# Sixteen more token rows through gathered down rows, and every second lower weight block split on VectorE

## The chip, the cores and the metric

The kernel runs on one core of a Trainium2 chip. Its time is device microseconds of one execution; before the change the median of three runs is 1582.86 us (1582.15 to 1584.1). The profiled execution took 1584.32 us, of which 1582.4 us lie between its first and its last instruction.

## The reference

One decoder layer over 512 tokens of width 1024: a mixer, cross-attention into 256 memory tokens, and a PEER channel mixer, in which each of 8 heads chooses 16 of 16384 single-neuron experts for every token. Nearly all that matters here is the last part:

```python
q = (tokens @ w_query).reshape(Ntok, PEER_HEADS, 2, PEER_DK)
s = jnp.einsum('nhpd,hpkd->nhpk', q, sub_keys)
s_top, i_top = lax.top_k(s, K)                       # K = 16 in each half
cand = (s_top[:, :, 0, :, None] + s_top[:, :, 1, None, :]).reshape(Ntok, PEER_HEADS, K * K)
best, pos = lax.top_k(cand, K)
gate = jax.nn.softmax(best, axis=-1)
u = jnp.take(expert_down, idx, axis=0)
a = jax.nn.gelu(jnp.einsum('nd,nhkd->nhk', xb, u), approximate=False)
v = jnp.take(expert_up, idx, axis=0)
out = jnp.einsum('nhk,nhkd->nd', gb * a, v)
```

## The kernel before, in words

The tokens lie in four tiles of 128. Up to the queries all four are treated alike. In the channel mixer the work is split by tokens.

**Dense tokens.** For the first three tiles without their last 32 rows (352 tokens, the constant DE) nothing is gathered. The products with all 16384 down rows are made, in 128 blocks of 128 experts, each 24 matmuls of 352 columns (8 chunks of the width, three products of a split into a high and a low half). GELU is applied to all of them, a dense table of gates, zero for what isn't chosen, multiplies them, and 128 blocks of the up matrix follow, again 24 matmuls of 352 columns each.

**Gathered tokens.** The fourth tile, and the 32 last rows of the third (the edge), fetch the rows that they chose, one token to a partition. A gather brings 128 rows (512 KB); the fourth tile needs 128 of them, the edge 32, with 4 slots to a token. VectorE then makes one dot product of each gathered tile with the tokens (the function dots, line 1250, result in dot3 or edge_dot).

**The stage of down blocks** is where the change works. It has three parts. In the first, 52 blocks (AHEAD), TensorE makes down blocks while VectorE chooses the experts of the three dense tiles, with dots in between: 18 to a tile, 54 in all. In the second, 44 steps (STEPS), each step is one block and one gate step of 24 small matmuls from one-hot tables that VectorE builds (the function hots); DOTS_STEP gives the dots of each step, 74 in all. In the third, the last 32 blocks, DOTS_END gives the dots still open, 32, one to a block for 22 blocks and then two.

**The order on each engine** is written out by hand. A down block passes through four engines: SyncE loads it into a ring of 5, ScalarE rounds it into a high half in a ring of 3 (the function high, line 603), GpSimd subtracts to get the low half (the function low, line 470), and TensorE waits for the low half (the function columns). Since the high ring has three places, ScalarE splits block i+2 only when block i-1 has been used, which is when block i begins. ScalarE also writes the GELU of each block (line 853, and line 952 for the last 24 blocks, which stay in SBUF; the others go out to DRAM and come back).

GpSimd does two things in one program order: the low halves, and the issue of the gathers (the function down_row, line 502). In the first part the tiles of gathered rows are a ring of 7, and GpSimd issues them at a set pace of 6 for 5 blocks. From the second part on the ring has 4 places, so gather k waits until dot k-4 is done, and GpSimd issues the gathers of block i right after the low half of block i, so that the last gather that it issues there needs the last dot that VectorE makes in the matching step.

ScalarE waits for VectorE's choice before blocks 15, 30 and 45 (EXP_AT), and TensorE turns the chosen numbers before blocks 36 and 51 (turn_indices).

**The stage of up blocks** has 128 blocks. VectorE multiplies the hidden values by the gates: 320 columns from a table that came back from DRAM (line 1474) and 32 from a table kept in SBUF (near, line 1478).

Of the kernel before, what the change touches and what calls it, by code (L numbers as in the profile page):

```python
# [8 lines left out]
U32 = mybir.dt.uint32  # L9
# [34 lines left out]
EXP_AT = (15, 30, 45)  # L44
PICKED_AT = 19
TURN_AT = (PICKED_AT + 4, 36, 52)
# [3 lines left out]
DE = DN - EDGE  # L50
STEPS = DE // TB
# [14 lines left out]
ROWS = SLOTS + EDGE_SLOTS  # L66
FIRST_EDGE = 32
LOWS = range(33, 40)
GEL_AT, SPLIT_AT, LAST_TURN = 12, 20, 28
# [17 lines left out]

def row_stream():
    stream, own, edge = [], 0, 0
    for k in range(ROWS):  # L90
        if edge < EDGE_SLOTS and k >= FIRST_EDGE:
            stream.append((True, edge))
            edge += 1
        else:
            stream.append((False, own))
            own += 1
    return stream
# [3 lines left out]
EDGE_DONE = FIRST_EDGE + EDGE_SLOTS  # L101

# [5 lines left out]
def build(nc, x_in, mem_in, vecs_in, final_in, ffn_in, front_w, keys_in, down_in, down_rows, up_in, up_pairs, out, gate_dram, hid_dram):  # L108
    ctx = ExitStack()
    with ctx:  # L110
# [110 lines left out]
        hid = [at(kb, DE) for kb in (137.25, 138.625, 18.5, 19.875)]  # L221
        hk_last, split_last = at(136.25, 2 * P, 2, P), at(26, 3 * P, 3, P)
        edge_idx, edge_dot, edge_gel = (at(kb, EDGE_SLOTS) for kb in (18, 18.125, 18.25))
        edge_gate, edge_w, edge_sum_of = (at(17.5 + 0.125 * j, EDGE_SLOTS) for j in range(3))
# [27 lines left out]
        hid_kept = [at(kb, DE) for kb in [108 + 1.5 * j for j in range(4)] + [156 + 1.5 * j for j in range(10)]  # L252
# [6 lines left out]
        hidr = at(60, 2 * PAIRS_IN * DE, 2 * PAIRS_IN, DE)  # L259
# [7 lines left out]
        low_ready = sem("low_ready")  # L267
# [53 lines left out]
        edge_moved, fin_squares = sem("edge_moved"), sem("fin_squares")  # L321
        mix_square, mix_last = sem("mix_square_of_third_tile"), sem("mix_last_tile")
# [123 lines left out]
        def _(pool):  # L446
# [45 lines left out]
            def down_row(k):  # L492
# [6 lines left out]
                edge, j = STREAM[k]  # L499
                if edge and j == 0:  # L500
                    pool.wait_ge(edge_moved, 2 * 16 * PARTS)
                nc.gpsimd.indirect_dma_start(ring[slot], None, down_rows, bass.IndirectOffsetOnAxis(  # L502
                    (edge_idx if edge else idx3)[:, j:j + 1].bitcast(U32), 0))\
# [59 lines left out]
        def _(act):  # L563
# [44 lines left out]

            def weight_high(i, s):
                act.wait_ge(w_raw, i * 2 + 2)  # L610
                nc.scalar.activation(wgt_half[0][:, s, 0:DE], wraw[:, s, 0:DE], ACT.Copy).then_inc(w_high, 1)
# [234 lines left out]
            def early_at(i):  # L846
# [6 lines left out]
                nc.scalar.activation(hid[i % HIDS], psum[:, 4 + i % 2, 0:DE], ACT.Gelu).then_inc(gelu_out, 1)  # L853
                act.wait_ge(gelu_out, i + 3)
                act.dma_start(hid_dram[i // 2, :, i % 2 * DE:(i % 2 + 1) * DE], hid[i % HIDS])\
# [23 lines left out]
            for n in range(DT):  # L879
                early_tiles((4 + PARTS, TURN_AT[0], TURN_AT[1])[n], EXP_AT[n])  # L880
# [10 lines left out]
                elif n == 1:  # L891
                    early_tiles(EXP_AT[n], TURN_AT[n])
# [15 lines left out]
            for n in range(STEPS):  # L908
# [3 lines left out]
                if n == GEL_AT:  # L912
                    act.wait_ge(dot_done, EDGE_DONE)
                    step(nc.scalar.activation(edge_gel, edge_dot, ACT.Gelu))
                    act.wait_ge(idx_ready, 3)
                if GEL_AT <= n < GEL_AT + PARTS:
# [25 lines left out]
            for j in range(KEEP):  # L942
# [9 lines left out]
                nc.scalar.activation(hid_kept[j][:, 0:DE], psum[:, 4 + i % 2, 0:DE], ACT.Gelu).then_inc(gelu_out, 1)  # L952
                if i == NK - 4:
                    act.wait_ge(dot_done, ROWS)
                    high_up(0, 0, 16)
# [4 lines left out]
                if i == NK - 2:  # L960
                    high_up(1, 1, 16)
                    weight_high(1, 1)
            for s in range(2, 4):
                high_up(s, s, 16)
                weight_high(s, s)
            for u in range(4, RING_U):
                act.wait_ge(up_done, u - 3)
                high_up(u, u, 16)
                weight_high(u, u % 4)
            with act.Fori(1, NK // RING_U) as r:  # L970
                for s in range(RING_U):
                    act.wait_ge(up_done, r * RING_U + (s - 3))
                    high_up(r * RING_U + s, s, r * 16 + 16)
                    weight_high(r * RING_U + s, s % 4)
# [37 lines left out]
        def _(dve):  # L1012
# [221 lines left out]
            def dots(first, count):  # L1234

                for k in range(first, first + count):
# [5 lines left out]
                    edge, j = STREAM[k]  # L1242
# [7 lines left out]
                    nc.vector.tensor_tensor_reduce(ring[slot], ring[slot], h_row, 1.0, 0.0, ALU.mult, ALU.add,  # L1250
                                                   (edge_dot if edge else dot3)[:, j:j + 1]).then_inc(dot_done, 1)
# [168 lines left out]
            for n in range(STEPS):  # L1420
# [4 lines left out]
                if n == SPLIT_AT:  # L1425
# [3 lines left out]
                                                     ident.rearrange("p (q t) -> p t q", q=PARTS), AX_X, ALU.add))  # L1429
                    step.end()  # L1430
# [5 lines left out]
            kd = dots(kd, ROWS - kd)  # L1436
# [29 lines left out]
            def weigh(i, landed, block, kept_hid=None):  # L1466
# [4 lines left out]
                else:  # L1471
# [7 lines left out]
                    wraw[:, s, FAR * CH:DE].rearrange("p (i n) -> p i n", i=1),  # L1479
                    h[:, FAR * CH:DE].rearrange("p (i n) -> p i n", i=1),  # L1480
                    near[:, block:block + 1, :], ALU.mult).then_inc(w_raw, 1)
# [65 lines left out]
        def _(pe):  # L1547
# [45 lines left out]
            def columns(b, rhs, n, bank):  # L1593

                pe.wait_ge(low_ready, b + 1)
# [447 lines left out]
```

## Time and profile before

| what | value |
|---|---|
| median of three runs | 1582.86 us |
| profiled execution | 1584.32 us |
| its span, first to last instruction | 1582.4 us |
| TensorE busy | 1565.8 us, 99% |
| VectorE busy | 1164.6 us, 74% |
| GpSimd busy | 963.6 us, 61% |
| ScalarE busy | 663.3 us, 42% |
| moved by DMA | 438.91 MB |

The profile shows one execution. PE is TensorE's matmuls, PEld its weight loads, DVE is VectorE, ACT ScalarE, POOL GpSimd, SP SyncE. A matmul's busy time is longer than its share of the array, since matmuls overlap: what one costs is read from the distance between starts. A time in square brackets behind a row is the idle time of that engine before it, and the name behind it is what ended it. psum, kept and arena are the large memories: kept and arena hold nearly every tile, so rows are told apart by their line.

### The profile page before, as it was taken

To read this page: it belongs to the slowest core of one execution; us is meant where nothing else is said; L and a number is where in the kernel's file an instruction comes from. 1 tells how busy PE (TensorE), PEld (TensorE's weight loads), DVE (VectorE), ACT (ScalarE), POOL (GpSimd) and SP (SyncE) were. 2 spreads that over 40 slices of the span, in tenths; PEclk is the share of its full clock that TensorE was granted. 3 is DMA by queue.
4 is the path that set the end of the run, shared out by engine and by line. 5 is a ranking of instruction groups with operands and counts; after the bars stand their busy time and mean duration, and the time that the engine had idled before them with its cause. 6 is when DMAs were issued, how large, how long until landed. Compare 5 with 4: busy or idle time off the path is not lost.

```text
span 1582.4 us, 26079 instructions
## 1 busy us (share of the span) xinstructions
PE 1565.8 (99%) x9937; PEld 1483.6 (94%) x9937; DVE 1164.6 (74%) x2263; ACT 663.3 (42%) x994; POOL 963.6 (61%) x555
## 2 busy tenths in 40 slices
PE   8999999999999999999999999999999999999997
PEld 6888888888989999999999999999999999999997
DVE  5155351251579999999999883338999999998995
ACT  5352452552434444444444544334334333333433
POOL 4463326523235899887778778876757665564741
PEclk9999999999999999999999999999999999999999
DMA  5232252313424999989999999879999999999981
GB/s 196 88 103 67 73 158 95 115 54 118 149 84 130 302 347 349 330 285 313 379 399 397 396 410 393 309 248 365 411 410 406 399 406 409 395 404 393 400 354 54
DMA packets 129697, 438.91 MB, mean 277 GB/s; under 512 B 13888, under 2 KB 28224, under 8 KB 121280
## 3 DMA queue, kind: packets, MB, share of 16 engines
q1 hardware_dynamic: 60592, 227.43, 39.6%
q0 software_dynamic: 46080, 167.79, 27.8%
q10 hardware_dynamic: 22928, 42.41, 7.0%
q8 instruction: 59, 0.97, 0.2%
q14 instruction: 38, 0.31, 0.1%
HBM read 395.21 MB, written 41.81 MB: 276 GB/s over the span
## 4 chain that ended last, share of the span: by engine, by line
PE 50%; DVE 4%; DMA 3%; issue 1%; POOL 1%; ACT 0%; ACTq 0%; POOLq 0%
PE psum L1589 16%; PE psum L1590 16%; PE psum L1591 16%; DMA arena<-down_rows,kept 3%; PE psum L1905 2%; DVE arena L1415 1%; DVE arena L1250 1%; POOL w_low L470 1%; POOL arena L502 0%; DVE arena L1410 0%; DVE arena L1411 0%; DVE arena L1323 0%; DVE kept L1375 0%; DVE arena L1383 0%; PE psum L1941 0%
## 5 line engine op out<-in xcount | busy, mean ns | idle before, releaser
L470 POOL TENSOR_TENSOR w_low<-kept,w_high 128x1024 fp32r<-128x1024 f32 x205 | 500.7, 2445 | 316.8 <-ACT w_high L603 306.1
L1589 PE MATMUL psum<-hT_high,w_high 128*128 128x352 f32 (+2 forms) x1392 | 477.6, 343 | 1.7 <-POOL w_low L470 1.7
L1591 PE MATMUL psum<-hT_high,w_low 128*128 128x352 f32 (+2 forms) x1392 | 470.6, 338 | 0.0
L1590 PE MATMUL psum<-hT_low,w_high 128*128 128x352 f32 (+2 forms) x1392 | 470.6, 338 | 0.0
L1590 PE MATMUL psum<-wgt_low,up_high 128*128 128x352 f32 x1016 | 330.0, 325 | 0.0
L1589 PE MATMUL psum<-wgt_high,up_high 128*128 128x352 f32 x1016 | 328.7, 324 | 0.0
L1591 PE MATMUL psum<-wgt_high,up_low 128*128 128x352 f32 x1016 | 327.5, 322 | 0.0
L603 ACT ACTIVATE w_high<-kept 128x1024 fp32r<-128x1024 f32 x211 | 222.6, 1056 | 129.6 <-PE psum L1591 91.2
L1589 PEld LDWEIGHTS psum<-hT_high,w_high 128*128 128x128 f32 x1392 | 262.1, 188 | 14.5 <-issue 2.9
L1590 PEld LDWEIGHTS psum<-hT_low,w_high 128*128 128x128 f32 x1392 | 262.3, 188 | 11.8 <-issue 0.5
L1591 PEld LDWEIGHTS psum<-hT_high,w_low 128*128 128x128 f32 x1392 | 262.0, 188 | 12.0
L1250 DVE CUSTOM_DVE_ANT_0 arena<-arena,psum 128x1024 f32<-128x1024 f32 x160 | 192.3, 1215 | 78.1 <-DMA arena<-down_rows,kept 77.5
L607 ACT ACTIVATE up_high<-arena 128x1024 fp32r<-128x1024 f32 x128 | 135.6, 1059 | 269.2 <-PE psum L1591 214.8
L550 POOL DMA_INDIRECT kept<-up_in,kept x100 | 175.7, 1757 | 103.3 <-DVE kept L1459 76.0
L502 POOL DMA_INDIRECT arena<-down_rows,kept x160 | 153.2, 958 | 68.9 <-DVE kept L1250 45.8
L1591 PEld LDWEIGHTS psum<-wgt_high,up_low 128*128 128x128 f32 x1016 | 193.0, 190 | 0.0
L1590 PEld LDWEIGHTS psum<-wgt_low,up_high 128*128 128x128 f32 x1016 | 191.1, 188 | 0.0
L1589 PEld LDWEIGHTS psum<-wgt_high,up_high 128*128 128x128 f32 x1016 | 190.5, 188 | 0.0
L1445 DVE TENSOR_TENSOR up_low<-arena,up_high 128x1024 fp32r<-128x1024 f32 x128 | 156.4, 1222 | 20.0 <-ACT up_high L607 19.8
L550 POOL DMA_INDIRECT arena<-up_in,kept x60 | 112.4, 1873 | 66.6 <-DVE kept L1459 48.3
L1459 DVE SCALAR_TENSOR_TENSOR kept<-kept 128x1024 f32<-128x1024 f32 x80 | 102.4, 1280 | 2.0
L1415 DVE TENSOR_TENSOR arena<-arena,psum 128x3072 bf16<-128x3072 bf16 x44 | 76.9, 1748 | 0.0
(285 smaller groups left out, 1957.3 us busy)
## 6 DMA issues: line engine op xcount, KB each, us to landing
kept<-down_in SPq DMA_DIRECT2D x128, 512.0 KB, 6.4
arena<-up_pairs SPq DMA_DIRECT2D x64, 1024.0 KB, 9.2
kept<-front_w SPq DMA_DIRECT2D x92, 512.0 KB, 3.5
gate_dram<-arena ACTq DMA_DIRECT2D x40, 512.0 KB, 11.0
arena<-hid_dram SPq DMA_DIRECT2D x52, 352.0 KB, 12.7
arena<-gate_dram SPq DMA_DIRECT2D x8, 1280.0 KB, 14.0
kept<-gate_dram SPq DMA_DIRECT2D x8, 1280.0 KB, 14.2
hid_dram<-arena ACTq DMA_DIRECT2D x52, 176.0 KB, 6.6
```

The costliest lines, as they stand in the source:

```text
L470: nc.gpsimd.tensor_tensor(lower, ring[:, p % RING, :], high.bitcast(F32), ALU.subtract).then_inc(low_ready, 1)
L502: nc.gpsimd.indirect_dma_start(ring[slot], None, down_rows, bass.IndirectOffsetOnAxis((edge_idx if edge else idx3)[:, j:j + 1].bitcast(U32 ...
L550: nc.gpsimd.indirect_dma_start(rows_c[k % RING_C], None, up_rows, bass.IndirectOffsetOnAxis(numbers.bitcast(U32), 0))\
L603: nc.scalar.activation(w_half(p)[0], ring[:, p % RING, :], ACT.Copy).then_inc(high_ready, 1)
L607: nc.scalar.activation(up_hi[:, s % 4, :], uraw[:, up_slot(s), :], ACT.Copy).then_inc(up_high, 1)
L1250: nc.vector.tensor_tensor_reduce(ring[slot], ring[slot], h_row, 1.0, 0.0, ALU.mult, ALU.add, (edge_dot if edge else dot3)[:, j:j + 1]).the ...
L1415: nc.vector.tensor_tensor(hot_g[:, s], hot_i.rearrange("p (n q) i r -> p n q i r", q=1).to_broadcast(each), pieces[:, m:m + PAIRS].rearran ...
L1445: nc.vector.tensor_tensor(up_lo[:, up_slot(s), :], uraw[:, up_slot(s), :], up_hi[:, s % 4, :].bitcast(F32), ALU.subtract).then_inc(up_low, 1)
L1459: ins = nc.vector.scalar_tensor_tensor(x[:, ST, :], row, w3[:, n:n + 1], x[:, ST, :], ALU.mult, ALU.add)
L1589: nc.tensor.matmul(out, lhs[0], rhs[0], start=first, stop=False)
L1590: nc.tensor.matmul(out, lhs[0], rhs[1], start=False, stop=False)
L1591: return nc.tensor.matmul(out, lhs[1], rhs[0], start=False, stop=last)
```

## The change

- 16 more rows of the third tile, those before the edge (called semi), get their down products from gathered rows. The down blocks now have 336 columns (DS) instead of 352. For these rows the gate times the GELU is formed beforehand (semi_gel into split_last), and goes through the gate table, so that their part of the weights is copied from the table by ScalarE (weights_tail), once per up block. The up blocks stay 352 columns wide.
- 16 more gathers and dots, 176 instead of 160. The stream is the first 32 of the fourth tile, then the edge's 32, then 16 of the semi rows, then the rest.
- The first part has 57 blocks instead of 52; a tile's choice has 21 dots instead of 18, so 63 in all. ScalarE's waits move to blocks 17, 33 and 50, TensorE's turns to blocks 40 and 56.
- The third part has 27 blocks. Its dots come as 2, 2, 1, repeated.
- In the third part the low halves of blocks 103, 105, ... 123 (LOWS_END, 11 of them) are made by VectorE (low_by_vector), each ahead of the dots of the step two blocks earlier; GpSimd leaves them out.
- ScalarE's loop over the up blocks is written out.

```diff
-EXP_AT = (15, 30, 45)
-PICKED_AT = 19
-TURN_AT = (PICKED_AT + 4, 36, 52)
+EXP_AT = (17, 33, 50)
+PICKED_AT = 21
+TURN_AT = (PICKED_AT + 4, 40, 57)
+SEMI = 16
+DS = DE - SEMI
-DOTS_CAND = (1, 1, 1, 1)
-DOTS_HOT = 6
+DOTS_CAND = (2, 2, 2, 2)
+DOTS_HOT = 5
-DOTS_END = (1,) * 22 + (2,) * 5
+DOTS_END = (2, 2, 1) * 7 + (2, 2)
+LOWS_END = range(DURING + 2, NK - 4, 2)
...
             for i in range(AHEAD + 2, NK):
-                low(FRONT + i)
+                if i not in LOWS_END:
+                    low(FRONT + i)
                 for _ in range(DOTS_STEP[i - AHEAD] if i < DURING else DOTS_END[i - DURING] if i - DURING < len(DOTS_END) else ROWS):
...
+            def weights_tail(i):
+                block = (i + SPILL) % NK
+                nc.scalar.activation(wraw[:, i % 4:i % 4 + 1, DS:DE], near[:, block:block + 1, NEAR - SEMI:NEAR], ACT.Copy)\
+                    .then_inc(tail_copied, 1)
...
                     elif k == EDGE_DONE:
                         dve.wait_ge(dot_done, k)
+                        dve.wait_ge(semi_moved, 2 * 16 * SEMI_PARTS)
+                        step.put(nc.vector.memset(semi_gel, 1.0))
+                        step(nc.vector.tensor_tensor(h_chunks, edge_h, ffn_row.rearrange("p (k n) -> p k n", k=KC), ALU.mult))
+                    elif k == SEMI_DONE:
+                        dve.wait_ge(dot_done, k)
                         step(nc.vector.tensor_copy(h_chunks, own_h))
...
-            kd = dots(kd, ROWS - kd)
+            def low_by_vector(b):
+                dve.wait_ge(high_ready, b + 1)
+                p = position(b)
+                high, lower = w_half(p)
+                nc.vector.tensor_tensor(lower, ring[:, p % RING, :], high.bitcast(F32), ALU.subtract).then_inc(low_end, 1)
+
+            for n, count in enumerate(DOTS_END):
+                if DURING + n + 2 in LOWS_END:
+                    low_by_vector(FRONT + DURING + n + 2)
+                kd = dots(kd, min(count, ROWS - kd))
...
             def first_product(i):
                 pe.wait_ge(gelu_out, i + 1)
-                columns(i + FRONT, hT_half, DE, 4 + i % 2)
+                columns(i + FRONT, hT_half, DS, 4 + i % 2)
```

GpSimd's order where the third part begins. Before, from the last step of the second part on (TENSOR_TENSOR is a low half, DMA a gather, x2 two in a row):

```order
L470 TENSOR_TENSOR w_low<-kept,w_high 128x1024 [waits high_ready]
L502 DMA arena<-down_rows,kept 128x1024 [waits dot_done] x2
L470 TENSOR_TENSOR w_low<-kept,w_high 128x1024 [waits high_ready]
L502 DMA arena<-down_rows,kept 128x1024 [waits dot_done]
L470 TENSOR_TENSOR w_low<-kept,w_high 128x1024 [waits high_ready]
L502 DMA arena<-down_rows,kept 128x1024 [waits dot_done]
```

And in the changed kernel, the low half of block 101, its two gathers, the low half of block 102, and so on:

```order
L477 TENSOR_TENSOR w_low<-kept,w_high 128x1024 [waits high_ready]
L511 DMA arena<-down_rows,kept 128x1024 [waits dot_done] x2
L477 TENSOR_TENSOR w_low<-kept,w_high 128x1024 [waits high_ready]
L511 DMA arena<-down_rows,kept 128x1024 [waits dot_done] x3
L477 TENSOR_TENSOR w_low<-kept,w_high 128x1024 [waits high_ready]
L511 DMA arena<-down_rows,kept 128x1024 [waits dot_done] x4
L477 TENSOR_TENSOR w_low<-kept,w_high 128x1024 [waits high_ready]
```

One low half in two is gone from GpSimd, and the gathers of two blocks stand together between the low halves that are left.

VectorE's order at the same place. Before, after the last one-hot tables, only dots follow (each dot is an ISA pair, the product and the reading of its sum):

```order
L1415 TENSOR_TENSOR arena<-arena,psum 128x3072 [waits dve_step]
L1250 ISA arena,kept<-arena,psum 128x1024 [waits ld_down_rows_b0]
L1250 ISA kept 128x1
L1250 ISA arena,kept<-arena,psum 128x1024 [waits ld_down_rows_b1]
L1250 ISA kept 128x1
L1250 ISA arena,kept<-arena,psum 128x1024 [waits ld_down_rows_b2]
```

In the changed kernel, behind the last tables and the two dots of their step: the low half of block 103, two dots (the step of block 101), two dots (block 102), the low half of block 105:

```order
L1482 TENSOR_TENSOR w_low<-kept,w_high 128x1024 [waits high_ready]
L1289 ISA arena,kept<-arena,psum 128x1024 [waits ld_down_rows_b2]
L1289 ISA kept 128x1
L1289 ISA arena,kept<-arena,psum 128x1024 [waits ld_down_rows_b3]
L1289 ISA kept 128x1
L1289 ISA arena,kept<-arena,psum 128x1024 [waits ld_down_rows_b0]
L1289 ISA kept 128x1
L1289 ISA arena,kept<-arena,psum 128x1024 [waits ld_down_rows_b1]
L1289 ISA kept 128x1
L1482 TENSOR_TENSOR w_low<-kept,w_high 128x1024 [waits high_ready]
```

A subtraction that waits for ScalarE's high half now stands ahead of the dots, and GpSimd's gathers wait for those dots.

## Rows read from the trace of the kernel before

**Rows 1.** TensorE's longest wait inside: us in total, times, longest.

```profile
PE psum L1589 <- POOL w_low L470: 1.9, 4, 1.1
```

**Rows 2.** By stretch (length, then PE, PEld, DVE, ACT, POOL busy, clock, DMA, GB/s).

```profile
513.30:715.00 201.70, 201.34 (x1262) 200.88 (x1261) 195.21 (x583) 90.29 (x119) 175.37 (x103) 1.00 0.93 321
715.00:949.80 234.80, 233.44 (x2118) 227.54 (x2117) 218.58 (x291) 112.54 (x179) 182.20 (x125) 1.00 1.00 384
949.80:1072.70 122.90, 122.90 (x773) 122.90 (x771) 43.78 (x73) 47.60 (x68) 100.51 (x60) 1.00 0.85 311
1072.70:1573.00 500.30, 499.99 (x3115) 499.36 (x3113) 464.35 (x675) 194.36 (x273) 291.82 (x164) 1.00 0.95 375
```

**Rows 3.** TensorE in order of time: starts of matmuls of 256 and 352 columns.

```profile
197.74 0.28 PE L1589 MATMUL psum<-memT_high,w_high 128*128 128x256 f32 x1
...
200.62 0.28 PE L1589 MATMUL psum<-memT_high,w_high 128*128 128x256 f32 x1
...
560.10 0.32 PE L1589 MATMUL psum<-hT_high,w_high 128*128 128x352 f32 x1
...
563.94 0.33 PE L1589 MATMUL psum<-hT_high,w_high 128*128 128x352 f32 x1
```

**Rows 4.** GpSimd, first part: five blocks with six gathers.

```profile
594.18 2.42 POOL L470 TENSOR_TENSOR w_low<-kept,w_high 128x1024 fp32r<-128x1024 f32 x1
...
613.29 2.41 POOL L470 TENSOR_TENSOR w_low<-kept,w_high 128x1024 fp32r<-128x1024 f32 x1
```

**Rows 5.** DMA issues, microseconds to landing, first between 590 and 610, then 670 and 690.

```profile
arena<-down_rows,kept POOLq DMA_INDIRECT x6, 6.1
...
arena<-down_rows,kept POOLq DMA_INDIRECT x6, 8.6
```

**Rows 6.** VectorE, third tile's choice: last dot among the candidates, end; TensorE's turn behind it.

```profile
685.54 0.08 DVE L1250 DVE_READ_ACCUMULATOR2_ANT kept<- 128x1 f32 x1
...
708.95 0.29 DVE L1377 TENSOR_TENSOR arena<-psum,arena 128x128 f32<-128x128 f32 x1
...
710.78 0.71 PE L1951 MATMUL psum<-kept,arena 128*128 128x128 f32 x5
```

**Rows 7.** VectorE, second part: its first table, and its first wait for TensorE.

```profile
712.65 0.36 DVE L1406 COPY psum<-arena 128x192 f32<-128x192 f32 x1 [3.40 <-ACT arena L876]
...
874.78 0.69 DVE L1410 TENSOR_TENSOR arena<-arena,psum 128x1024 bf16<-128x1024 bf16 x1 [3.33 <-PE psum L1905]
```

**Rows 8.** A dot, and the low half behind the gather that waits for it.

```profile
841.06 1.22 DVE L1250 CUSTOM_DVE_ANT_0 arena<-arena,psum 128x1024 f32<-128x1024 f32 x1
...
843.52 2.42 POOL L470 TENSOR_TENSOR w_low<-kept,w_high 128x1024 fp32r<-128x1024 f32 x1
```

**Rows 9.** Third part: a GELU, and the low half behind the next high half.

```profile
1000.14 0.46 ACT L952 ACTIVATE arena<-psum 128x352 f32<-128x352 f32 x1 [2.43 <-PE psum L1591]
...
1001.62 2.41 POOL L470 TENSOR_TENSOR w_low<-kept,w_high 128x1024 fp32r<-128x1024 f32 x1 [0.34 <-ACT w_high L603]
```

**Rows 10.** Late low half, the block that waited for it, and its GELU.

```profile
657.98 2.41 POOL L470 TENSOR_TENSOR w_low<-kept,w_high 128x1024 fp32r<-128x1024 f32 x1
...
660.54 0.40 PE L1589 MATMUL psum<-hT_high,w_high 128*128 128x352 f32 x1 [0.36 <-POOL w_low L470]
...
664.67 0.47 ACT L853 ACTIVATE kept<-psum 128x352 f32<-128x352 f32 x1 [2.46 <-PE psum L1591]
```

**Rows 11.** VectorE's subtraction of the same shape, all 128 in the up blocks.

```profile
L1445 DVE TENSOR_TENSOR up_low<-arena,up_high x128: 1211/1221/1274, 1063.8 to 1553.7; 128x1024 fp32r<-128x1024 f32 x128
```

**Rows 12.** The granted clock (after the five engines) behind TensorE's last matmul (1572.39, 0.55 long).

```profile
1575.00:1575.50 0.50, 0.00 (x0) 0.00 (x0) 0.47 (x3) 0.17 (x1) 0.00 (x0) 0.91 0.00 0
1575.50:1576.00 0.50, 0.00 (x0) 0.00 (x0) 0.27 (x2) 0.44 (x3) 0.00 (x0) 0.50 0.00 0
```

**Rows 13.** One VectorE line without and with a low half running on GpSimd (563.05 to 565.46).

```profile
493.54 0.29 DVE L1294 TENSOR_TENSOR arena<-arena 128x128 f32<-128x128 f32 x1
...
563.11 2.50 DVE L1294 TENSOR_TENSOR arena<-arena 128x128 f32<-128x128 f32 x1
```

More of the change, by code:

```diff
@@ L85 @@
 SPILL = NK - KEEP
+OWN, AT_EDGE, IN_SEMI = range(3)
 def row_stream():
[L89 to L97, printed above, removed]
+    middle = [(AT_EDGE, j) for j in range(EDGE_SLOTS)] + [(IN_SEMI, j) for j in range(SEMI_SLOTS)]
+    own = [(OWN, j) for j in range(SLOTS)]
+    return own[:FIRST_EDGE] + middle + own[FIRST_EDGE:]
 STREAM = row_stream()
 EDGE_DONE = FIRST_EDGE + EDGE_SLOTS
+SEMI_DONE = EDGE_DONE + SEMI_SLOTS
 V_MIX, V_CONV, V_HGRN, V_LB0, V_LB1, V_ATT, V_MEM, V_FFN, V_CW = 0, 8, 12, 16, 20, 24, 32, 40, 48
@@ L251, in build @@
         near = at(172, P * NEAR, P, NEAR)
[L252 removed]
+        hid_kept = [at(kb, DS) for kb in [108 + 1.5 * j for j in range(4)] + [156 + 1.5 * j for j in range(10)]
                     + [202 + 1.375 * j for j in range(4)] + [114] + [133 + 1.375 * j for j in range(5)]]
@@ L891, in _ @@
                 elif n == 1:
-                    early_tiles(EXP_AT[n], TURN_AT[n])
+                    act.wait_ge(edge_moved, 2 * 16 * PARTS)
+                    for q in range(SEMI_PARTS):
+                        if q % 2 == 0:
+                            early_at(EXP_AT[n] + q // 2)
+                        act.dma_start(semi_idx[q * SEMI:(q + 1) * SEMI, :],
+                                      idx_last[SEMI0:E0, q * SEMI_SLOTS:(q + 1) * SEMI_SLOTS]).then_inc(semi_moved, 16)
+                    early_tiles(EXP_AT[n] + SEMI_PARTS // 2, TURN_AT[n])
                     act.wait_ge(hk_tr, 1)
@@ L915, in _ @@
                     act.wait_ge(idx_ready, 3)
+                if n == SEMI_AT:
+                    act.wait_ge(dot_done, SEMI_DONE)
+                    act.wait_ge(semi_moved, 2 * 16 * SEMI_PARTS)
+                    step(nc.scalar.activation(semi_dot, semi_dot, ACT.Gelu))
+                if SEMI_AT <= n < SEMI_AT + SEMI_PARTS // 2:
+                    for q in (2 * (n - SEMI_AT), 2 * (n - SEMI_AT) + 1):
+                        act.dma_start(semi_gel[SEMI0:E0, q * SEMI_SLOTS:(q + 1) * SEMI_SLOTS],
+                                      semi_dot[q * SEMI:(q + 1) * SEMI, :]).then_inc(semi_moved, 16)
                 if GEL_AT <= n < GEL_AT + PARTS:
@@ L960, in _ @@
                 if i == NK - 2:
+                    weights_tail(1)
                     high_up(1, 1, 16)
                     weight_high(1, 1)
[L963 to L968, printed above, removed]
-                weight_high(u, u % 4)
[L970 to L974, printed above, removed]
+            for u in range(2, NK):
+                if u >= 4:
+                    act.wait_ge(up_done, u - 3)
+                weights_tail(u)
+                high_up(u, u % RING_U, 16 * (u // RING_U + 1))
+                weight_high(u, u % 4)
             act.preload_act_table_set("natural_log_exp_and_others")
@@ L1593, in columns @@
             def columns(b, rhs, n, bank):
-                pe.wait_ge(low_ready, b + 1)
+                if b - FRONT in LOWS_END:
+                    pe.wait_ge(low_end, LOWS_END.index(b - FRONT) + 1)
+                else:
+                    pe.wait_ge(low_ready, b + 1 - sum(i < b - FRONT for i in LOWS_END))
                 for k in range(KC):
```

57 lines of the change are left out of this document (39 added, 18 removed).

## The prediction

> **What bounds the kernel now.** I read the stretches first. Of the four that matter, TensorE is busy for all but 0.4 us of the first part of the down blocks, all but 1.4 us of the second, the whole third and all but 0.3 us of the up blocks, at a granted clock of 1.00 [rows 2]. Its longest wait in total on another engine is 1.9 us in four pieces, for low halves from GpSimd [rows 1]. So TensorE's columns are the bound, and a thinner block is worth its columns if the others keep up. The same rows show how near they are: VectorE is busy 195 of 202 us and GpSimd 175 in the first part, VectorE 219 of 235 us in the second with the DMA engines at 1.00. Only in the third is VectorE idle (44 of 123 us), while GpSimd is at 101 [rows 2]. A change that adds dots and gathers therefore has to be followed through the orders of GpSimd and VectorE, which I did next in the order of time.
>
> **The columns saved.** From one 352 column matmul to the 24th behind it 3.84 us pass, 160 ns each; for 256 columns it is 2.88 us, 120 ns each [rows 3]. That is 40 ns for 96 columns, so 16 columns are worth 6.67 ns, and a down block falls from 3.84 to 3.68 us. 128 blocks of 24 matmuls: -20.5 us. The up blocks keep their width: 0.
>
> **First part, 57 blocks.** GpSimd takes 19.11 us for five low halves and six gathers (594.18 to 613.29) [rows 4]. TensorE took 19.2 for five blocks and will want 18.4. The pace of gathers is unchanged (6 for 5 blocks, now until block 53), so GpSimd becomes the slower one by 0.7 us in five blocks; it starts with a lead that I estimate at 1.5 us and TensorE begins to wait near block 22. That alone is 31 blocks x 0.14 = 4.3 us by block 53. The later end is VectorE's. Block 22's low half starts at 594.18 now [rows 4] and, being set by GpSimd's own pace, at about 593 then. The last gather that the third tile's candidates need is number 57 (of 0 to 62); by the pace it stands behind block 49's low half, 27 x 3.82 = 103.2 us later, so it is issued near 698.7. It lands 6.1 us later, or 8.6 as in the busier window [rows 5]; with the dot (1.14) that is 706.0 to 708.5. From the end of the last candidates' dot to the last piece of the choice now pass 23.7 us (685.54 to 709.24) [rows 6], with one dot fewer 22.5. So TensorE's second turn can begin at 728.5 to 731. Now it begins at 710.78 [rows 6]; five more blocks of 3.68 less 51 x 0.16 make 721.0. The part costs 7.5 to 10 us. Below, if gathers land early and VectorE alone sets the pace: nine dots more are 10.3 us, the blocks give 10.2, cost 0. I take 7.6. ScalarE's added DMA issues and the moved waits (blocks 17, 33, 50) hide beside TensorE's block, 0.
>
> **Second part, 44 steps.** TensorE's step falls by 0.16 us from 5.285 (a 3.84 us block and the gate products) to 5.125. VectorE started its first table at 712.65 and never waited for TensorE until 871.45, step 31 [rows 7]: 158.8 us for 31 steps, 5.12 us each, DMA waits included. It has no reserve left against 5.125, and gets more: the product for the semi rows (1.2 us, the copy behind it stands already in the old kernel), a fill and a small product, 1.6 us together. The same bytes in 3% less time meet DMA engines that are full at 384 GB/s [rows 2]. Bounds: 0, and 8 us (the whole 7 us of this part's columns given back, and the fill). I take 3.
>
> **Third part, the place that decides.** By the order, GpSimd issues the gathers of block i behind its low half and ahead of the next one; each needs the dot four places before it, so the last one needs the last dot of VectorE's matching step. In the changed kernel VectorE puts the low half of block i+2 ahead of exactly those dots, when i is odd (101 to 121). That subtraction needs the high half of block i+2, which ScalarE makes only when block i begins, since the high ring has three places. So for odd i the low half of block i+1 can't begin before a chain has run that starts with block i itself:
> - TensorE's block started at 660.54 and its GELU at 664.67 [rows 10], 0.29 us after the 3.84 us of the block; so the GELU of block i-1 begins 0.29 us after block i.
> - From a GELU's start to an instruction that waited for the next high half: 1.48 us (1000.14 to 1001.62) [rows 9].
> - VectorE's subtraction: 1.22 us. The trace doesn't show one on down weights; the same shape in the up blocks is 1.211 to 1.274 [rows 11].
> - From the start of a dot to the start of the low half behind its gather: 2.46 us (841.06 to 843.52) [rows 8]. With two dots in the step the second starts 1.14 us later.
> - The low half itself 2.41, and 0.15 until TensorE starts (660.39 to 660.54) [rows 10].
>
> Sum: 8.01 us with one dot, 9.15 with two, from the start of block i to that of block i+1, where 3.68 would do. Of the 11 odd blocks, steps 2, 8, 14 and 20 have one dot and the other seven two: 4 x 4.33 + 7 x 5.47 = 55.6 us. Even blocks don't wait, since VectorE's half is ready long before. The dots behind VectorE's subtraction find their rows landed, as their gathers were issued a pair of blocks (12 us) ahead. Behind each stall stand ScalarE's splits and SyncE's loads, which wait for used blocks, so nothing else catches up. The bounds: 50 (chain a tenth shorter) and 64.
>
> **The clock.** TensorE stands still 4.3 to 5.5 us eleven times. The only row on this is at the end: the granted clock left 1.00 between 1575.0 and 1575.5 and was 0.50 behind it, 2.1 to 2.6 us after the last matmul's end at 1572.94 [rows 12]. So I expect it to fall to the lower of its levels (1.2 GHz) in these stalls. A block wholly there costs 336/1.2 GHz less 336/2.4 GHz, 24 times: 3.36 us more. It hurts only behind the stall, because the chain runs beside the block ahead of it. Bounds 0 and 37 us; no row shows how soon it rises again, and I take 0.4 of the upper one, 15 us.
> The Trainium skill (TensorE: Matmul & The Clock Gate, HAM oscillation) says that a kernel which waits for a transfer between bursts of matmuls starts every burst at the low clock. Its whole bursts at that level would make the 15 us up to 37 and the time 1666; the trace has one such fall, and no rise.
>
> **The rest.** ScalarE copies a 128x16 tail for each up block; it is busy 194 of 500 us there [rows 2], 0. VectorE's product is 16 columns shorter, 0 beside TensorE. The loop written out: 0.
>
> **Sum.** 1584.3 (the profiled execution: span 1582.4 and 1.9 around it) - 20.5 + 7.6 + 3 + 55.6 + 15 = 1645.0. That execution was 1.5 us above the median shown, so on the median: 1643.5, said as 1644.
>
> **Rivals.**
> - The clock holds in the stalls, all else as above: 1644 - 15 = 1629. For it, the fall took over 2 us; against it, the stalls are twice as long. It is inside my range, 0.2 of the 0.82.
> - VectorE's subtraction also waits for GpSimd's: a VectorE line with two inputs took 2.50 us instead of 0.29 when it met a low half [rows 13]. With 2.4 us more for each of the 11, 1644 + 26 = 1670. Against it: at that place GpSimd waits for the dots, so no low half is running. The Trainium skill (GPSIMD Engine Reference, Specifications) has the two engines share their SBUF interfaces, with contention for VectorE instructions with two SBUF inputs. By that rule the move of lows to VectorE pays for every overlap; the trace agrees. Chance 0.05.
> - The chain isn't closed: GpSimd gets past the gathers of block i before VectorE's dots, or the high half comes a block earlier. The place is the low half of block 102 and its ten successors, and the price is the whole 55.6 and the clock's 15. It decides from a chain of 3.68 + (20.5 - 10.6)/11 = 4.6 us: shorter, and the kernel is faster. Then 1582.9 - 20.5 + 10.6 = 1573. For it: TensorE is never held in this part now, and GpSimd has 22 us free in it [rows 2]. Against it: the printed orders, and a ring of four with gathers always four ahead. 0.09; with the first and second part hidden as well it is 1562, 0.02.
> - It isn't slower but the gain is spent: chains near 4.6 us, or a full DMA queue holding the dots. 1583, 0.02.
>
> **The numbers.** Forecast 0.82, 1644, with a range of its own of 1624 to 1668; rivals 0.05, 0.11 (faster) and 0.02. The case at 1573 is left out of the range as its one side, at the other side what is above 1668: 1620 to 1668. About 0.2% (3 us) is what a measurement of this kernel tells from no change. Faster 0.11, same 0.02, slower 0.87.
>
> **What would show it.** In the changed profile: starts of 336 column matmuls 153.3 ns apart; TensorE's wait for w_low in the stretch of blocks 101 to 122 near 56 us in 11 pieces of 4 to 6 us, alternate blocks; in the same stretch POOL's gathers waiting for VectorE and VectorE's subtraction waiting for ScalarE's high half; a granted clock there well under 1.00; in the first part four or five us of small waits for w_low, and a turn that begins 7 us late for its columns. Wrong it is if the third part of 27 blocks takes about 100 us, or if TensorE's waits there come from gathers that haven't landed.

## The result, and the profile after

The changed kernel takes 1654.58 us (median of four runs, 1652.59 to 1655.51), the kernel before 1583.39 us in the same session: 1.0449 times as long, 95% interval 1.0431 to 1.0467. The forecast was 1644 us and slower. The profiled execution of the changed kernel has a span of 1652.5 us, 70.1 us more than before.

The stretches of the changed kernel, cut at the ends of the same parts as in [rows 2] (length, then busy time of PE, PEld, DVE, ACT, POOL, granted clock, DMA share, GB/s):

```profile
514.00:737.80 223.80, 216.60 (x1383) 214.10 (x1382) 198.66 (x598) 97.43 (x130) 195.95 (x116) 0.98 0.95 326
737.80:967.30 229.50, 226.36 (x2117) 220.89 (x2116) 216.73 (x290) 113.72 (x181) 179.04 (x122) 1.00 1.01 390
967.30:1143.70 176.40, 123.27 (x651) 120.53 (x650) 64.71 (x102) 39.69 (x60) 71.53 (x54) 0.84 0.65 221
1143.70:1643.00 499.30, 499.05 (x3111) 498.65 (x3109) 462.50 (x673) 206.80 (x398) 257.40 (x163) 1.00 0.94 374
```

In the third part TensorE now stands still for 53 of 176 us, at a clock of 0.84; before it was busy for the whole part at 1.00. All engines idle more there, and the DMA engines fall from 0.85 to 0.65: no engine is short of capacity, each waits for another in a ring. The up blocks are unchanged. The first part is longer too, 223.8 us for 57 blocks.

The waits of the third part (us in all, times, longest); the last line answers to [rows 1]:

```profile
ACT arena L989 <- PE psum L1643: 113.9, 20, 10.5
DVE w_low L1482 <- ACT w_high L613: 100.6, 11, 10.9
POOL arena L511 <- DVE kept L1289: 90.8, 16, 9.8
...
PE psum L1641 <- POOL w_low L477: 53.1, 11, 5.4
```

Read as a circle: VectorE's subtraction waits for ScalarE's high half, GpSimd's gathers (L511) for VectorE's dots, TensorE for GpSimd's low half, and ScalarE for TensorE. One turn of it, in order of time (start, duration, engine, line, what ended the idle time before):

```profile
1011.81 0.45 ACT L989 ACTIVATE arena<-psum 128x336 f32<-128x336 f32 x1 [10.43 <-PE psum L1643]
1012.16 1.05 ACT L613 ACTIVATE w_high<-kept 128x1024 fp32r<-128x1024 f32 x1
...
1013.24 1.23 DVE L1482 TENSOR_TENSOR w_low<-kept,w_high 128x1024 fp32r<-128x1024 f32 x1 [10.85 <-ACT w_high L613]
1014.39 1.21 DVE L1289 CUSTOM_DVE_ANT_0 arena<-arena,psum 128x1024 f32<-128x1024 f32 x1
...
1015.53 1.22 DVE L1289 CUSTOM_DVE_ANT_0 arena<-arena,psum 128x1024 f32<-128x1024 f32 x1
...
1015.88 0.93 POOL L511 DMA_INDIRECT arena<-down_rows,kept  x1 [9.85 <-DVE kept L1289]
...
1017.11 0.94 POOL L511 DMA_INDIRECT arena<-down_rows,kept  x1 [0.30 <-DVE kept L1289]
1018.07 2.35 POOL L477 TENSOR_TENSOR w_low<-kept,w_high 128x1024 fp32r<-128x1024 f32 x1
...
1020.57 0.62 PE L1641 MATMUL psum<-hT_high,w_high 128*128 128x336 f32 x1 [5.11 <-POOL w_low L477]
```

The odd block's 24 matmuls start from 1011.61, 0.20 us ahead of the first row, to 1015.15; then TensorE stands until 1020.57. The chain, from block start to block start, is 8.96 us, forecast 9.15. In intervals between starts (each less the 153.3 ns of a running matmul) the eleven pieces are 5.39, 5.29, 5.27, 5.27, 4.04, 5.27, 5.28, 4.04, 5.28, 5.52 and 4.29 us: 54.9 us.

The clock over the same turn (columns as above):

```profile
1011.00:1015.30 4.30, 4.30 (x29) 4.18 (x27) 2.06 (x2) 1.40 (x2) 0.00 (x0) 0.97 0.43 122
1015.30:1018.00 2.70, 0.16 (x2) 0.00 (x0) 2.70 (x7) 1.40 (x2) 1.82 (x2) 1.00 0.47 147
1018.00:1020.50 2.50, 0.00 (x0) 0.00 (x0) 1.03 (x2) 0.00 (x0) 2.40 (x2) 0.51 0.98 349
1020.50:1024.50 4.00, 3.93 (x14) 3.96 (x15) 0.00 (x0) 0.00 (x0) 1.89 (x2) 0.50 0.71 223
1024.50:1026.50 2.00, 2.00 (x14) 2.00 (x13) 0.00 (x0) 0.01 (x1) 0.00 (x0) 0.91 0.72 225
```

TensorE stops at 1015.5; at 1018 the clock falls to 0.50 (1.2 GHz) and matmuls then start 280 ns apart, until 1024.9. Fifteen of the 24 matmuls of the even block pay 0.13 us each. Over the eleven turns the matmuls that are slow lose 21.9 us, 1.5 to 2.9 behind each stall.

First part: TensorE waits ahead of block 35 and again ahead of block 52; ScalarE's waits of blocks 33 and 50 stand ahead of just these blocks' high halves. The choice of the second tile, and what ScalarE does behind it:

```profile
643.90 0.29 DVE L1333 TENSOR_TENSOR arena<-arena 128x128 f32<-128x128 f32 x1
...
644.23 0.31 ACT L905 ACTIVATE arena<-arena 128x128 f32<-128x128 f32 x1 [4.10 <-DVE arena L1333]
644.45 1.04 ACT L613 ACTIVATE w_high<-kept 128x1024 fp32r<-128x1024 f32 x1
...
645.57 2.35 POOL L477 TENSOR_TENSOR w_low<-kept,w_high 128x1024 fp32r<-128x1024 f32 x1 [2.68 <-ACT w_high L613]
...
648.07 0.95 POOL L511 DMA_INDIRECT arena<-down_rows,kept  x1
```

ScalarE's exponential (L905) has its fixed place ahead of a high half. Each choice has four more dots ahead of this point than before; ScalarE stands 4.10 us, and the high half, GpSimd's low half and TensorE's block are all late: TensorE loses 2.25 us here and 2.71 ahead of block 52, and a slow clock behind each (0.53 from 649.4 to 653.0, 0.61 from 718 to 722) costs another 1.5. TensorE's turn of the third tile's numbers (before the change in [rows 6]) begins at

```profile
733.04 0.71 PE L2006 MATMUL psum<-kept,arena 128*128 128x128 f32 x5
```

where the columns alone would allow 721.0. The row has no idle time before it: TensorE came to its turn late, and VectorE's last piece, at 731.53, no longer held it.

### The profile page after: what moved, and what is told of

It reads as the page before. It is cut to its first block, busy times and chain, and to the rows that moved or that the text cites. A ratio compares the mean times of both kernels' runs of the same rounds, so it can differ in the third digit from the quotient of the medians.

```text
span 1652.5 us, 26094 instructions
## 1 busy us (share of the span) xinstructions
PE 1574.0 (95%) x9937; PEld 1487.5 (90%) x9937; DVE 1186.3 (72%) x2309; ACT 676.2 (41%) x1123; POOL 918.4 (56%) x560
## 4 chain that ended last, share of the span: by engine, by line
PE 72%; DVE 9%; POOL 8%; DMA 5%; issue 3%; ACT 2%; ACTq 0%; SPq 0%; DVEq 0%; POOLq 0%
PE psum L1641 22%; PE psum L1642 22%; PE psum L1643 22%; POOL w_low L477 6%; DMA arena<-down_rows,kept 4%; DVE arena L1289 3%; POOL arena L511 3%; DVE arena L1454 2%; PE psum L1960 1%; ACT w_high L613 1%; PE psum L1909 1%; DVE w_low L1482 1%; PE psum L1937 1%; PE psum L1666 1%; DVE arena L1449 1%
## 5 line engine op out<-in xcount | busy, mean ns | idle before, releaser
L477 POOL TENSOR_TENSOR w_low<-kept,w_high 128x1024 fp32r<-128x1024 f32 x194 | 474.2, 2447 | 312.7 <-ACT w_high L613 302.1
L1641 PE MATMUL psum<-hT_high,w_high 128*128 128x336 f32 (+2 forms) x1392 | 482.3, 346 | 63.5 <-POOL w_low L477 63.3
L1642 PE MATMUL psum<-hT_low,w_high 128*128 128x336 f32 (+2 forms) x1392 | 472.9, 340 | 0.0
L1643 PE MATMUL psum<-hT_high,w_low 128*128 128x336 f32 (+2 forms) x1392 | 472.6, 340 | 0.0
L1641 PEld LDWEIGHTS psum<-hT_high,w_high 128*128 128x128 f32 x1392 | 270.8, 195 | 81.1 <-issue 64.4
L1642 PEld LDWEIGHTS psum<-hT_low,w_high 128*128 128x128 f32 x1392 | 270.9, 195 | 11.9 <-issue 0.5
L511 POOL DMA_INDIRECT arena<-down_rows,kept x176 | 168.8, 959 | 154.1 <-DVE kept L1289 129.0
L1289 DVE CUSTOM_DVE_ANT_0 arena<-arena,psum 128x1024 f32<-128x1024 f32 x176 | 209.1, 1214 | 27.1 <-DMA arena<-down_rows,kept 23.7
L560 POOL DMA_INDIRECT kept<-up_in,kept x100 | 154.9, 1549 | 122.9 <-DVE kept L1511 92.8
L560 POOL DMA_INDIRECT arena<-up_in,kept x60 | 99.0, 1650 | 81.4 <-DVE kept L1511 58.4
L621 ACT ACTIVATE arena<-arena 128x16 f32<-128x16 f32 x128 | 27.3, 214 | 224.8 <-PE psum L1643 222.1
```

Of the source, the lines that this page charges most:

```text
L477: nc.gpsimd.tensor_tensor(lower, ring[:, p % RING, :], high.bitcast(F32), ALU.subtract).then_inc(low_ready, 1)
L560: nc.gpsimd.indirect_dma_start(rows_c[k % RING_C], None, up_rows, bass.IndirectOffsetOnAxis(numbers.bitcast(U32), 0))\
L1641: nc.tensor.matmul(out, lhs[0], rhs[0], start=first, stop=False)
L1642: nc.tensor.matmul(out, lhs[0], rhs[1], start=False, stop=False)
L1643: return nc.tensor.matmul(out, lhs[1], rhs[0], start=False, stop=last)
```

## The experiments

In the expectations "theory order" is the mechanism of the forecast. All times are medians, with the ratio to the kernel before on the same chip.

| kernel | us | ratio, 95% interval |
|---|---|---|
| changed | 1654.6 | 1.0449 (1.0431 to 1.0467) |
| low_behind_dots | 1598.9 | 1.0093 (1.007 to 1.0115) |
| gathers_behind_low | 1601.3 | 1.0111 (1.0071 to 1.015) |
| lows_back | 1595.2 | 1.0071 (1.0054 to 1.0088) |
| few_lows_behind | 1595.7 | 1.0089 (1.0061 to 1.0117) |
| dots_left_out | 1578.1 | 0.9969 (0.995 to 0.9988) |
| warm | 1633.1 | 1.0309 (1.0291 to 1.0326) |
| before_vector_lows | 1649.1 | 1.0411 (1.0393 to 1.0428) |
| exp_later | 1653.2 | 1.0437 (1.042 to 1.0455) |
| columns_alone | 1573.4 | 0.9939 (0.9923 to 0.9956) |

**The order alone.** Two lines change places in VectorE's queue:

```diff
-                if DURING + n + 2 in LOWS_END:
-                    low_by_vector(FRONT + DURING + n + 2)
                 kd = dots(kd, min(count, ROWS - kd))
+                if DURING + n + 2 in LOWS_END:
+                    low_by_vector(FRONT + DURING + n + 2)
```

> The changed kernel, with VectorE's low half put behind the dots of its step instead of ahead of them. Every instruction stays on its engine. Theory order: the 54.9 us for which TensorE stands still in the third part (11 pieces), and the 21.9 us of slow matmuls behind them, come from the subtraction standing ahead of dots whose gathers GpSimd has queued ahead of its own low half. They all go: 1654.6 - 76.8 = 1577.8 us (1574 to 1585), wait for w_low in the third part under 6 us, granted clock there 1.00. Rival engine: VectorE's subtraction is too dear for the place whatever its order (two more instructions' worth of VectorE time, shared memory access with GpSimd): TensorE keeps at least 40 us of the waits, 1635 us or more.

1598.9 us: 55.7 us go by the order alone, so the eleven stalls are the order's and not the engine's. But 21 us more than expected stay, and the time lies outside the range given. Three lines of the waits between 967 and 1090 us, and VectorE's subtraction (count, min/median/max ns):

```profile
POOL arena L511 <- DVE kept L1289: 31.5, 15, 3.7
DVE arena L1289 <- DMA arena<-down_rows,kept: 18.5, 14, 3.1
PE psum L1641 <- POOL w_low L477: 15.1, 6, 7.0
```

```profile
L1482 DVE TENSOR_TENSOR w_low<-kept,w_high x11: 1222/1465/3547, 969.5 to 1063.9; 128x1024 fp32r<-128x1024 f32 x11
```

Six waits instead of eleven, and of another kind: GpSimd waits for dots, and dots now wait for rows that haven't landed (in the changed kernel that was 2.0 us in this part). And the subtraction took up to 3.5 us where it ran beside a low half of GpSimd's: the one at 969.53 ended at 973.08, 1.1 us behind GpSimd's (969.58 to 971.98).

**The low halves back on GpSimd**, all dots kept:

```diff
-LOWS_END = range(DURING + 2, NK - 4, 2)
+LOWS_END = range(0)
```

> The changed kernel with all low halves of the end given back to GpSimd (LOWS_END empty); the additional dots and gathers stay. Theory order: the 11 long stalls go (-76.8 us). GpSimd then has for three blocks 3 low halves of 2.41 and 5 gathers of 0.95 us with gaps of 0.16 to 0.3, about 12.5 us where three blocks take 11.04, so it falls behind by 0.5 us a block: over 22 blocks 10.7 us, less a lead of about 2 us: 1577.8 + 9 = 1587 us (1578 to 1590), in many small waits. Rival: the additional dots are the cause, not the order; then the long stalls stay and it is 1635 us or more.

1595.2 us, 8 above the expectation and outside its range. The long stalls are gone; what is left are eleven waits, in all 12.2 us and none over 2.0, and a clock that still falls behind the two longest. Between 967 and 1090 us:

```profile
DVE arena L1289 <- DMA arena<-down_rows,kept: 53.9, 33, 5.6
PE psum L1641 <- POOL w_low L477: 12.2, 11, 2.0
```

**GpSimd's order mended instead.** In a step whose low half VectorE makes, GpSimd holds its gathers back until its own next low half is issued:

```diff
                 if i not in LOWS_END:
                     low(FRONT + i)
+                if i in LOWS_END:
+                    held = DOTS_END[i - DURING]
+                    continue
...
+                if i - 1 in LOWS_END:
+                    rows_now += held
```

> The changed kernel with GpSimd's order mended instead of VectorE's: in a step whose low half VectorE makes, GpSimd issues the gathers behind its own next low half instead of ahead of it. VectorE keeps the low half ahead of its dots. With the dots ahead of the low half (the run before this) 19 us of stalls were left, the longest 7.1 us, where GpSimd's low half stood behind gathers that waited for dots that waited for their rows. Theory queue: what holds TensorE is always GpSimd's low half behind gathers that aren't yet allowed; here two gathers' worth of time lies between: third part within 3 us of 99.5, so 1654.6 - 76.8 = 1578 us (1576 to 1584). Rival gathers: the ring of four rows with some 5 us from issue to landing can't feed 39 dots in these 22 blocks at any order; then about as low_behind_dots, 1590 us or more.

1601.3 us: most of the stalls go by this repair too, so the circle needed both orders. But 17.4 of 54.9 us stay, in seven pieces, the longest 5.4 us. The theory of the queue as the only limit falls, and the time is the rival's. Whether rows that land late are the reason, as the rival has it, isn't shown: VectorE's subtraction is slow here too, and no run separates the two.

```profile
L1488 DVE TENSOR_TENSOR w_low<-kept,w_high x11: 1212/1350/3940, 970.1 to 1065.0; 128x1024 fp32r<-128x1024 f32 x11
```

**The load.** What is left after either repair should then be the 16 additional rows. Here the last 16 gathers and dots are left out (their results are missing), so the third part has 23 dots instead of 39:

```diff
-DOTS_END = (2, 2, 1) * 7 + (2, 2)
-LOWS_END = range(DURING + 2, NK - 4, 2)
+DOTS_END = (1,) * 23
+LOWS_END = range(0)
+DOTS_MADE = ROWS - 16
```

> The changed kernel with all low halves of the end on GpSimd, as in lows_back, and one dot and one gather a step there instead of 2, 2, 1; the last 16 of the 176 dots and gathers are left out (their activations are missing). In lows_back the third part has 18 us of gaps and in the two mended orders 20 to 27. Theory load: these are the price of the 16 additional rows themselves (0.5 MB each, 8.4 MB, where the DMA engines are at 1.0 until 990 us, and 0.95 us of GpSimd each): without them GpSimd needs 3.66 us a block, no gap over 1 us is left, and the time is 1654.6 - 76.8 = 1578 us (1575 to 1581). Rival: the narrower block itself is too fast for loads or high halves in this part; then it stays at 1590 us or more.

1578.1 us, as expected: 17.2 us less than lows_back, whose low halves stand on the same engine. The third part to its end, answering to the third row of [rows 2]:

```profile
967.30:1066.00 98.70, 96.59 (x630) 96.34 (x630) 31.79 (x52) 37.91 (x58) 80.13 (x46) 1.00 0.81 299
```

None of the orders tried has the sixteen gathers and dots for less than these 17 us. Which share of it is GpSimd's 0.95 us for each gather, which the DMA engines and which the ring of four rows, these runs don't separate.

**A mix meant to be the best**, every fourth low half by VectorE behind the dots, and the exponentials a block later:

```diff
-EXP_AT = (17, 33, 50)
+EXP_AT = (17, 34, 51)
-LOWS_END = range(DURING + 2, NK - 4, 2)
+LOWS_END = range(DURING + 2, NK - 4, 4)
-                if DURING + n + 2 in LOWS_END:
-                    low_by_vector(FRONT + DURING + n + 2)
                 kd = dots(kd, min(count, ROWS - kd))
+                if DURING + n + 2 in LOWS_END:
+                    low_by_vector(FRONT + DURING + n + 2)
```

> The changed kernel with a mix meant to be the best order: VectorE makes every fourth low half of the end (6, not 11) and behind the dots of its step, GpSimd the others; the exponentials stand one block later as in exp_later. Theory load: GpSimd has 16 low halves and 37 gathers in 22 blocks, some 83 us where 81 are to be had, and the gathers still need 5 to 10 us to land while the DMA engines are full; 15 us of gaps or less in the third part instead of 18 to 25, and 1.4 us from the exponentials: 1590 us (1583 to 1597), not faster than the kernel before. Rival order: with GpSimd neither overloaded nor behind a waiting gather the gaps go, 1577 us, faster than before.

1595.7 us, within the range given and no better than lows_back. No version with all 176 products was found that beats the kernel before.

**The clock by itself.** 24 matmuls that nothing reads, in the stalls of the changed kernel:

```diff
             for i in range(DURING, NK):
                 first_product(i)
+                if i + 1 < NK - 4 and (i - DURING) % 2 == 0 and i > DURING - 1:
+                    for _ in range(24):
+                        nc.tensor.matmul(psum[:, 3, 0:DS], hT_half[0][:, 0, 0:P], hT_half[0][:, 0, 0:DS], start=True, stop=True)
```

> The changed kernel with 24 additional matmuls of 336 columns, into a PSUM bank that is free there and whose result nothing reads, behind each odd block from 101 to 121. They run in the first 3.7 us of the 4.0 to 5.4 us stalls, so the chain is as long as before. Theory clock: the slow matmuls behind the stalls (intervals of 280 ns instead of 153) are there because TensorE stood still; the 21.9 us go, the stalls (as seen from the blocks) stay 55 us: 1632.7 us (1630 to 1637), granted clock 1.00 throughout. Rival: the clock falls for another reason (power of the other engines, DMA): no change, 1654 us.

1633.1 us, 21.5 less. The third part until 1122 us, where the changed kernel had 0.84:

```profile
967.30:1122.00 154.70, 140.89 (x891) 137.91 (x891) 63.40 (x99) 38.27 (x58) 70.31 (x52) 0.99 0.71 244
```

Stalls and clock are thereby measured apart: 55 and 22 us.

**One part of the change alone**, in the kernel before (352 columns, one dot a step):

```diff
 DOTS_END = (1,) * 22 + (2,) * 5
+LOWS_END = range(DURING + 2, DURING + 24, 2)
...
+            for n, count in enumerate(DOTS_END):
+                if DURING + n + 2 in LOWS_END:
+                    low_by_vector(FRONT + DURING + n + 2)
+                kd = dots(kd, min(count, ROWS - kd))
```

> The kernel before, 352 columns and one dot a step in the end, with one part of the change alone: every second low half (11 of them) by VectorE ahead of the dots of the step. Theory order: each pair of blocks has the chain with one dot; the changed kernel shows a stall of 4.04 us for it with a block of 3.68, so 3.88 with a block of 3.84: 11 x 3.88 = 43 us, and 1.6 us of slow clock behind each, 18 us: 1583.4 + 61 = 1644 us (1630 to 1650). Rival: it takes the second dot of a step to make the stall; with one dot, VectorE and GpSimd keep up, 1583 to 1590 us.

1649.1 us, 65.9 more than before. Between 950 and 1130 us:

```profile
POOL arena L503 <- DVE kept L1252: 102.7, 11, 10.9
...
PE psum L1602 <- POOL w_low L471: 43.7, 11, 4.8
```

The same circle with eleven turns: the last six stalls are 3.86 to 3.88 us as expected, the five ahead of them 3.99 to 4.93; together 45.4 us, and the slow matmuls 21.4 (1.6 to 1.7 behind eight of them, 2.5 to 2.7 behind three). So one edit, with no dot and no column changed, loses 65.9 us where the whole change loses 71.2.

**The exponentials.** EXP_AT = (17, 34, 51), and nothing else.

> The changed kernel with ScalarE's exponentials of the second and third choice behind one more block (EXP_AT 34 and 51 instead of 33 and 50), nothing else. In the trace ScalarE stands 4.1 us there for VectorE's candidates, its next high half is late, and TensorE loses 2.25 and 2.71 us and 1.5 us of slow clock behind each, 8.0 us. Theory wait: the two stalls go, but VectorE's end of the choice (731.8 in the trace, and TensorE's turn at 733.0) then is the bound of this part: the turn comes 1.2 to 2 us earlier, and no more; 1653 us (1651 to 1654.5). Rival: the stalls are the loss itself, and VectorE is late only because its gathers were held up by them: all 8 us come back, 1646.6 us.

1653.2 us; the 1.4 us less are within the spread of the runs. Both stalls are gone from the trace (one of 1.0 us comes a little later), and the wait stands in another place. VectorE's last piece and TensorE's turn behind it:

```profile
729.40 0.29 DVE L1416 TENSOR_TENSOR arena<-psum,arena 128x128 f32<-128x128 f32 x1
...
729.75 0.77 PE L2006 MATMUL psum<-kept,arena 128*128 128x128 f32 x5 [3.30 <-DVE arena L1416]
```

With ScalarE's wait out of the way, VectorE's choice is the next bound of the first part. The rival has a share too: the last piece comes 2.1 us earlier than in the changed kernel (729.40 against 731.53), so the old order had held VectorE up as well. The turn comes 3.3 us earlier, more than the 1.2 to 2 expected. Little of it arrives: the clock falls behind the new wait too (0.66 from 731 to 736), and the first stall of the third part begins 0.9 us earlier (969.72 against 970.59).

**The columns by themselves.** The kernel before with narrower down blocks; the products of 16 rows are left out.

```diff
-                columns(i + FRONT, hT_half, DE, 4 + i % 2)
+                columns(i + FRONT, hT_half, DE - 16, 4 + i % 2)
```

> The kernel before, with down blocks of 336 columns instead of 352 and nothing else (the products of 16 rows of the last tile are left out, so their gates' inputs are missing; no dot, gather, low half or wait is added or moved). Theory VectorE: the columns are worth 20.5 us for TensorE, but in the first part VectorE's choice ends at 709.24 and lets the turn come only about 1.5 us earlier than 710.78, which gives 6.7 of 8.2 us back, and in the second part VectorE needs 5.12 us a step as TensorE does, a loss of 0 to 3: 1583.3 - 20.5 + 6.7 + 1.5 = 1571 us (1569 to 1574). Rival columns: all of them are worth their time, 1563 us.

1573.4 us: 10.0 of 20.5 us arrive. The turn and VectorE's first table, which stood at 710.78 and 712.65 [rows 6, 7]:

```profile
708.96 0.71 PE L1951 MATMUL psum<-kept,arena 128*128 128x128 f32 x5
```

```profile
710.83 0.36 DVE L1406 COPY psum<-arena 128x192 f32<-128x192 f32 x1 [2.33 <-ACT arena L876]
```

Fifty-one blocks that are 8.2 us shorter move the turn by 1.8. The time is what the theory of VectorE foretold, but the trace doesn't bear out its reason. VectorE's last piece ended at 708.50, and the turn has no idle time before it. TensorE had lost its time earlier, in eight pieces of 0.5 to 1.2 us, 6.3 us together. One of them (1.2 us) is a wait for VectorE, at the turn of the tile before. The seven others, 5.1 us, each end 0.15 us behind a low half of GpSimd's, also where the row names another engine (ahead of one of them, of 1.2 us, GpSimd had itself waited 2.4 us for a dot):

```profile
593.72 2.41 POOL L470 TENSOR_TENSOR w_low<-kept,w_high 128x1024 fp32r<-128x1024 f32 x1
...
596.28 0.39 PE L1589 MATMUL psum<-hT_high,w_high 128*128 128x336 f32 x1 [0.56 <-ACT arena L853]
```

The next such low halves start at 612.88 and 632.00: GpSimd keeps its 19.1 us for five blocks [rows 4], where TensorE now wants 18.4.

## Why the prediction was right, and where a term was off

The forecast for the profiled execution was 1645.0 and 1654.4 came (span and 1.9 around it), 9.4 us more. By its own terms:

- **Columns, -20.5.** Right: starts of 336 column matmuls are 153.3 ns apart (24 of them in 3.68 us). What the others let through of it was in the next terms.
- **First part, +7.6 taken (7.5 to 10).** Measured 11.9: intervals above a running matmul's add up to 14.55 us, before 2.61. This term was mis-sized. GpSimd's pace is there as said (six small waits, 3.4 us in all, forecast 4.3). But "ScalarE's added DMA issues and the moved waits (blocks 17, 33, 50) hide beside TensorE's block, 0" failed: they cost 2.25 and 2.71 us. The forecast had the turn held by VectorE's choice, with an end at 728.5 to 731. VectorE's last piece was at 731.5, but TensorE had by then lost so much that it didn't wait at the turn; it did in exp_later (3.30 us), where the two stalls are gone. The new cost is 3.0 us of slow clock, which the forecast reckoned with in the third part only: a stall of 2.25 us was enough.
- **Second part, +3 taken (0 to 8).** About 2, by subtraction of the other terms; the stretch is 5.3 us shorter (229.5 against 234.8), where the columns alone are worth 7.0. The right size.
- **Third part, +55.6.** Measured 54.9. Alternate blocks from 102, eleven pieces, and the three waits of the circle were as foreseen. Eight steps were long and three short, not seven and four: in the second pair ScalarE issued two stores ahead of the high half (hidden values 0.34 us, gates 0.63), and this chain with one dot was 1.25 us longer than the next one. That the sum came within 1 us is in part luck: the usual stall was 5.28 us with two dots and 4.04 with one, forecast 5.47 and 4.33 (of the chain's parts, the start of the GELU was 0.20 us behind the block's, not 0.29), and the longer step made up for some of it.
- **Clock, +15 (0 to 37).** Measured 21.9, and 21.5 by warm: 0.6 of the upper bound instead of 0.4. The largest error of the sum. The share of 0.4 rested on no row. The only row had been a fall, none a rise [rows 12]; the rise came 3.2 to 6.3 us after the first matmul behind a stall. The Trainium skill (TensorE: Matmul & The Clock Gate, HAM oscillation) has each burst behind such a wait start at the low clock. The trace agrees for nine of the eleven; behind the two stalls of 4.04 us the burst started at 1.00, and the clock fell in it (at 1035.1 for the one of 1034.00).

The rivals. That the clock holds (1629) is refuted; warm makes that case by force and gives 1633. That the chain isn't closed (1573), or near 4.6 us a turn (1583), is refuted by the circle. That VectorE's subtraction pays for GpSimd's (1670) didn't happen here: the eleven took 1.224 to 1.226 us, since GpSimd waited for the dots just then. But in the mended orders it took up to 3.5 and 3.9 us. The Trainium skill (GPSIMD Engine Reference, Specifications) states the shared SBUF interfaces behind this, and the runs agree as soon as the two meet.

Open is how the 17 us of the sixteen rows divide over their three causes, and whether an order exists that pays less.

## What to carry to other kernels

Before an instruction is moved to a less busy engine, write down what stands behind it in that engine's queue and who waits for that: an instruction which must wait for the current block, put ahead of work that another engine needs for the next block, closes a circle, and each turn costs what its length exceeds the block by, however idle the engines are (77 us here with the clock, and 66 for the same edit in the kernel before). Reckon stalls of TensorE with the slow matmuls behind them; here that was 1.5 to 2.9 us for each 4 to 5.5 us. And when a narrower block saves columns, ask in each part who is second: here half of the saving was taken back before any work had been added, 5.1 us of it in the first part where TensorE waited for GpSimd's low halves, though VectorE had seemed the fuller engine there.

## What the runs showed of the hardware that was not expected

- The granted clock can fall after TensorE has resumed: after the stall from 1029.81 to 1034.00 it was still 1.00 for a us of matmuls, then 0.50 until 1038.5 (the changed kernel, columns as in the stretches):

```profile
1029.50:1034.00 4.50, 0.63 (x5) 0.38 (x4) 3.06 (x6) 1.39 (x2) 3.30 (x2) 1.00 0.59 174
1034.00:1035.00 1.00, 1.00 (x6) 1.00 (x7) 0.00 (x0) 0.00 (x0) 0.95 (x1) 1.00 0.62 246
1035.00:1035.50 0.50, 0.50 (x5) 0.50 (x4) 0.00 (x0) 0.00 (x0) 0.23 (x1) 0.62 0.19 74
1035.50:1038.50 3.00, 3.00 (x12) 3.00 (x12) 0.00 (x0) 0.00 (x0) 0.71 (x1) 0.50 0.84 228
```

- Matmuls whose result nothing reads, in the first 3.7 us of a stall, kept it at 0.99 over the part.
- A VectorE subtraction of 128x1024 with two inputs took 1.22 us alone and up to 3.94 us beside GpSimd's of the same shape (2.4 us): it waited the other out. The longest, in gathers_behind_low, started at 1056.52 and ended at 1060.46, 1.1 us behind the low half that GpSimd made from 1056.97 to 1059.37.
- With the DMA engines at 1.0, gathered rows landed 9 to 12 us after the issue of their gathers (in low_behind_dots issued at 974.49, 975.75 and 976.99, their dots at 983.49, 986.95 and 989.36, each of which had waited for them; the DMA share was 1.03), where the quieter stretch of [rows 5] has 6.1.
